# Retention stage: split products for the weighing, tiles long and short by turns, turning and gating one step later

## Chip, cores and metric

One Trainium2 chip, one core. The time is the device time of one execution in microseconds, of the program that computes three layers of a network for 1024 tokens. The change touches one stage of it, the retention.

## What is computed

For each of four heads, q and k (1024 x 256) are projected from the normed input and rotated, v (1024 x 512) is projected, and a gate g likewise. Then:

```python
s = einsum('qd,kd->qk', q, k) * gamma_h ** (t_q - t_k)    # for t_k <= t_q, else 0; k scaled by 256 ** -0.5
y = s @ v
y = (y - mean(y)) * rsqrt(var(y) + 1e-6)                  # per row of 512
y = y * silu(g)
```

The reference works in chunks of 128 with a carried state; the kernel computes the same sum over all earlier tokens directly. All inputs are fp32.

## The kernel before

The stage is `retention_stage`. Each head is a round: projections of q, k, v and gate (TensorE, as *split products*: an operand a is held as a_hi, rounded to fp32r, and a_lo = a - a_hi, and a product is three fp32r matmuls, hi*hi, hi*lo, lo*hi, in `product`, lines 773 to 781); then the scores and the weighing; and then the next head. GpSimd splits the arriving weights in slots (`w_split`, lines 730 and 732). Tokens are in eight tiles of 128.

In the weighing part, with key tile j and query tile i:

- `scores(j)` (L2914) multiplies key tile j with all queries from tile j on, in fp32, up to 512 columns at a time, into banks 0 and 1 or 2 and 3 of PSUM. VectorE's `decay(j)` (L3031) multiplies them by the decay table into the fp32 buffer `weights`. An fp32 matmul shows as two records in the trace.
- The weighing of query tile i (L2938) is i + 1 fp32 matmuls of 512 columns into bank 6 or 7. The tiles go in order, from one block to eight.
- VectorE takes the row statistics (L3050, L3054, L3056), ScalarE the root by Ln and Exp (L2980, L2982), VectorE a Newton step (L3061 to L3067) and the normed rows `yn` (L3072). TensorE turns them (`turn_y`, L2923) into bank 4 or 5, VectorE multiplies by the gate (`gated_out`, L3037) into `yT`. ScalarE stores `yT` at the end of the head.
- TensorE's order per head: scores 0 and 1, then for each tile i its weighing, scores i + 2, and the turn of tile i - 1; after tile 7, the first part of the next head's q projection (`narrow`, L777 to L781), and behind that the turn of tile 7. In VectorE's step i: statistics, decay(i + 2), Newton, normed rows of i, gate-out of i - 1.

In the last head, ScalarE (`rows_hi`, L2592), GpSimd (`rows_lo`, L2596) and SP's queue (`rows_load`) also bring the rows of the first two heads back in for the output projection, one k tile at a time in two buffers; before them GpSimd splits the next stage's first two weight slots (L2841, L2843). Engines run their queues in order and wait on counting semaphores. All wait counts are written by hand.

Of the kernel before, what the change touches and what calls it, by code (L numbers as in the profile page):

```python
# [85 lines left out]
def program(nc, x, positions, attn_norm_g, w_in, q_a_norm_g, w_q_b, kv_a_norm_g, w_kv_b, sb_out_norm_g,  # L86
# [2705 lines left out]
    def retention_stage(stage, weight, w, after):  # L2792
# [8 lines left out]
        tmp = sb("tmp", [P, 2, HALF])  # L2801
# [7 lines left out]
        yT = sb("yT", [P, NV, SEQ])  # L2809
        off = [sum((TT - i) * P for i in range(j)) for j in range(TT + 1)]  # L2810
        PA = sb("weights", [P, off[TT]])
# [3 lines left out]
        S = [ps[:, 0:2, :].rearrange("p b c -> p (b c)"), ps[:, 2:4, :].rearrange("p b c -> p (b c)")]  # L2815
        block = nc.Block()
        with block:
            @block.sync
            def _(sp):
                sp.dma_start(COS[:], tables["ret_cos"]).then_inc(gain_in.sem, 16)  # L2820
                sp.dma_start(SIN[:], tables["ret_sin"]).then_inc(gain_in.sem, 16)
                w_load_all(sp, w, RET_HEADS, per, ret_unit(weight), True)

                sp.wait_ge(w_lo.sem, w_lo.at(RET_HEADS * per + w.slots))
                for u in range(w.slots):
                    for dst, src in after(0, u)(w.raw[:, u, :]):
                        sp.dma_start(dst, src).then_inc(w_raw[u].sem, 16)
                sp.wait_ge(stored.sem, stored.at(16 * 2))
                rows_load(sp, ROWS)
# [19 lines left out]
            def _(pe):  # L2849
# [16 lines left out]
                for it in range(RET_HEADS):  # L2866
                    for u in range(1, 4):
                        if it and u == 2:

                            pe.wait_ge(y_out.sem, y_out.at(TT * it))  # L2870
                        narrow(it, u)

                    def values(u):

                        w_arrived(pe, w, it, per, u)
                        s = u % w.slots
                        for kk in range(2):
# [24 lines left out]

                    def scores(j):

                        if j < 2:

                            pe.wait_ge(dense_out.sem, dense_out.at(16 * it + 8 + 2 * j + 2))
                        else:
                            pe.wait_ge(decayed.sem, decayed.at(TT * it + j - 1))
                        n = (TT - j) * P  # L2910
                        for c0 in range(0, n, HALF):
                            c1 = min(c0 + HALF, n)
                            for i in range(2):
                                last = nc.tensor.matmul(S[j % 2][:, c0:c1], K[:, i, j * P:j * P + P],  # L2914
                                                        Q[:, i, j * P + c0:j * P + c1], start=i == 0, stop=i == 1)
                        last.then_inc(scores_ready.sem, 1)

                    def turn_y(i):
                        pe.wait_ge(normed.sem, normed.at(TT * it + i + 1))
                        if i >= 2:  # L2920
                            pe.wait_ge(y_out.sem, y_out.at(TT * it + i - 1))
                        for c in range(NV):
                            last = nc.tensor.transpose(ps[:, 4 + i % 2, c * P:c * P + P],  # L2923
                                                       YN[:, i % 2, c * P:c * P + P], ident[:])
                        last.then_inc(y_turned.sem, 1)

                    scores(0)
                    scores(1)
                    for i in range(TT):
                        pe.wait_ge(decayed.sem, decayed.at(TT * it + i + 1))  # L2930
                        if i == 0:
                            pe.wait_ge(dense_out.sem, dense_out.at(16 * it + 16))
                        if i >= 2:

                            pe.wait_ge(normed.sem, normed.at(TT * it + i - 1))
                        for j in range(i + 1):
                            at = off[j] + (i - j) * P
                            last = nc.tensor.matmul(ps[:, 6 + i % 2, :], PA[:, at:at + P], V[:, j, :],  # L2938
                                                    start=j == 0, stop=j == i)
                        last.then_inc(pv_done.sem, 1)  # L2940
                        if i + 2 < TT:
                            scores(i + 2)
                        if i >= 1:
                            turn_y(i - 1)
# [6 lines left out]
            def _(act):  # L2951
                for it in range(RET_HEADS):
                    act.dma_start(DEC[:], tables["decay"][bass.ds(it, 1), :, :].rearrange("a p c -> (a p) c"))\
                        .then_inc(table_in.sem, 16)
                    for i, t in enumerate(TOKENS):
                        act.wait_ge(dense_done.sem, dense_done.at(24 * it + 8 + i + 1))
                        nc.scalar.activation(V[:, t, :], ps[:, t, :], ACT.Copy).then_inc(dense_out.sem, 1)
                    for j in range(NV):
# [15 lines left out]
                        nc.scalar.activation(GE[:], GE[:], ACT.Ln, bias=1.0).then_inc(gate_exp.sem, 1)  # L2974
                        act.wait_ge(gate_step.sem, gate_step.at(2 * (NV * it + j) + 1))
                        nc.scalar.activation(GE[:], GE[:], ACT.Exp).then_inc(gate_exp.sem, 1)
                    for i in range(TT):
# [4 lines left out]
                        nc.scalar.activation(st[:, 10:11], st[:, 9:10], ACT.Exp, scale=-0.5).then_inc(root.sem, 1)  # L2982
                        for k in ROWS_AT[i] if it == RET_HEADS - 1 else ():
# [3 lines left out]
                    act.dma_start(YT[bass.ds(it * NV, NV), :, :].rearrange("a p t -> p a t"), yT[:])\  # L2987
# [3 lines left out]
            def _(dve):  # L2991
                dve.wait_ge(gain_in.sem, gain_in.at(32))
                with dve.Fori(0, RET_HEADS) as it:
# [29 lines left out]

                    for j in range(NV - 1):
# [3 lines left out]
                    def decay(j):  # L3028
                        n = (TT - j) * P
                        dve.wait_ge(scores_ready.sem, scores_ready.at(TT * it + j + 1))  # L3030
                        nc.vector.tensor_tensor(PA[:, off[j]:off[j] + n], S[j % 2][:, 0:n], DEC[:, 0:n], ALU.mult)\  # L3031
                            .then_inc(decayed.sem, 1)

                    def gated_out(i):
                        at = slice(i * P, i * P + P)
                        dve.wait_ge(y_turned.sem, y_turned.at(TT * it + i + 1))
                        nc.vector.tensor_tensor(yT[:, :, at], ps[:, 4 + i % 2, :].rearrange("p (v c) -> p v c", c=P),  # L3037
                                                GT[:, :, at], ALU.mult).then_inc(y_out.sem, 1)

                    decay(0)  # L3040
                    decay(1)
                    gate(NV - 1)

                    dve.wait_ge(stored.sem, stored.at(16 * it))
                    for i in range(TT):
                        st = stat[:, i, :]
                        o = ps[:, 6 + i % 2, :]
# [9 lines left out]
                        if i + 2 < TT:  # L3057
                            decay(i + 2)
# [15 lines left out]
                        if i >= 1:  # L3074
                            gated_out(i - 1)
# [10 lines left out]
        for m in (scores_ready, decayed, pv_done, ln_done, root, normed, y_turned, y_out):  # L3086
# [98 lines left out]
```

## Time and profile before

| | us |
|---|---|
| three runs, median (lowest, highest) | 3862.47 (3861.24, 3871.61) |
| the profiled execution | 3866.34 |
| its span | 3864.6 |
| mean granted TensorE clock | 0.966 |

The profile is of one execution. Times in the trace count from the start of its span. In a line of the timeline stand start, length, engine, line of the kernel, operation and tiles, and in brackets the idle time ahead and what ended it; several equal instructions in a row are merged (x16). The length of a matmul's record is longer than the distance to the next one, since matmuls are pipelined.

### The profile page before, as it was taken

How to read it: one execution, taken by the hardware profiler on the slowest of the kernel's cores; microseconds unless marked ns; L12 is line 12 of the kernel's file. 1: busy time of each engine (PE TensorE's matmuls, PEld its weight loads, DVE VectorE, ACT ScalarE, POOL GpSimd, SP SyncE). 2: the span in 40 equal slices, each digit the busy share in tenths (PEclk: the TensorE clock that was granted, in tenths of full speed). 3: DMA queues.
4: the chain of work that ended last, by engine and by line, in shares of the span. 5: the costliest groups of instructions: out<-in, count | busy, mean ns of one | idle time of the engine just before them, and what ended most of it. 6: DMA issues, size and time to landing. Idle time of an engine off the chain costs nothing. (4 is left out here: it accounts for less than half of the span.)

```text
span 3864.6 us, 48135 instructions
## 1 busy us (share of the span) xinstructions
PE 3640.7 (94%) x17390; PEld 2977.0 (77%) x17390; DVE 1636.6 (42%) x3174; ACT 1322.1 (34%) x2439; POOL 1387.1 (36%) x813
## 2 busy tenths in 40 slices
PE   7987798999999998999999999997899999999997
PEld 6776577878888886788888888886787776868686
DVE  4666445233333334465665655555103323241412
ACT  4777143111111113455555556656101203020300
POOL 3210300233333321455655665666322121313331
PEclk9997899999999998999999999998999999999998
DMA  3000201111111104342322432221413120202231
GB/s 93 23 6 6 52 31 65 45 60 50 49 50 48 46 27 92 41 57 47 52 55 47 37 41 39 36 36 50 147 33 110 33 66 28 71 23 76 92 127 70
DMA packets 200885, 208.25 MB, mean 54 GB/s; under 512 B 12360, under 2 KB 155759, under 8 KB 200703
## 3 DMA queue, kind: packets, MB, share of 16 engines
q1 hardware_dynamic: 181134, 154.70, 17.9%
q10 hardware_dynamic: 19568, 50.93, 3.7%
q8 instruction: 138, 2.26, 0.2%
q14 instruction: 45, 0.36, 0.0%
HBM read 174.08 MB, written 31.52 MB: 53 GB/s over the span
## 5 line engine op out<-in xcount | busy, mean ns | idle before, releaser
L777 PE MATMUL ps<-all_u_hi,kept_w_hi 128*128 128x512 f32 x1824 | 731.9, 401 | 21.7 <-POOL kept_w_lo L732 14.2
L781 PE MATMUL ps<-all_u_hi,kept_w_lo 128*128 128x512 f32 x1824 | 715.4, 392 | 0.0
L780 PE MATMUL ps<-all_u_lo,kept_w_hi 128*128 128x512 f32 x1824 | 714.2, 392 | 0.0
L730 POOL CAST kept_w_hi<-kept_w_raw 128x1024 fp32r<-128x1024 f32 x120 | 129.6, 1080 | 1396.5 <-PE ps L777 741.5
L1437 POOL TENSOR_SCALAR even_probs<-even_probs,even_stat 128x128 f32<-128x128 f32 (+7 forms) x256 | 450.8, 1769 | 295.4 <-DVE even_stat L1861 295.0
L777 PEld LDWEIGHTS ps<-all_u_hi,kept_w_hi 128*128 128x128 f32 x1824 | 347.0, 190 | 85.5 <-POOL kept_w_lo L732 14.4
L781 PEld LDWEIGHTS ps<-all_u_hi,kept_w_lo 128*128 128x128 f32 x1824 | 345.2, 189 | 74.5
L780 PEld LDWEIGHTS ps<-all_u_lo,kept_w_hi 128*128 128x128 f32 x1824 | 346.2, 190 | 63.4
L1866 DVE TENSOR_TENSOR even_probsT_lo<-ps,even_probsT_hi 128x512 fp32r<-128x512 f32 (+3 forms) x384 | 196.0, 551 | 262.8 <-ACT even_probsT_hi L1701 261.7
L1692 ACT ACTIVATE even_probs<-even_probs,even_stat 128x128 f32<-128x128 f32 (+7 forms) x256 | 199.1, 778 | 300.9 <-DVE even_stat L1855 300.9
L732 POOL TENSOR_TENSOR kept_w_lo<-kept_w_raw,kept_w_hi 128x1024 fp32r<-128x1024 f32 x120 | 294.5, 2454 | 9.6
L777 PE MATMUL ps<-kept_w_hi,all_u_hi 128*128 128x512 f32 x640 | 252.7, 395 | 8.3 <-DVEq L2673 8.3
L780 PE MATMUL ps<-kept_w_lo,all_u_hi 128*128 128x512 f32 x640 | 252.1, 394 | 0.0
L781 PE MATMUL ps<-kept_w_hi,all_u_lo 128*128 128x512 f32 x640 | 251.9, 394 | 0.0
L2758 ACT ACTIVATE mlp_relu<-ps 128x512 f32<-128x512 f32 x64 | 38.3, 598 | 575.4 <-PE ps L781 575.4
L1701 ACT ACTIVATE even_probsT_hi<-ps 128x512 fp32r<-128x512 f32 (+3 forms) x384 | 167.7, 488 | 50.6 <-PE ps L1553 41.4
L2782 DVE TENSOR_TENSOR residual<-ps,residual 128x512 f32<-128x512 f32 x128 | 87.4, 692 | 229.5 <-PE ps L781 229.5
L1553 PE MATMUL ps<-all_ident,even_probs 128*128 128x128 f32 x1152 | 164.8, 281 | 16.9 <-POOL even_probs L1437 12.8
L2684 DVE TENSOR_TENSOR residual<-ps,residual 128x512 f32 x48 | 32.7, 692 | 344.7 <-PE ps L781 344.7
L1553 PEld LDWEIGHTS ps<-all_ident,even_probs 128*128 128x128 f32 x1152 | 136.2, 144 | 33.1 <-POOL even_probs L1437 16.1
L1533 PE MATMUL ps<-even_k_hi_hi,even_q_hi_lo 128*128 128x512 f32 (+2 forms) x384 | 145.9, 382 | 6.5 <-DVE even_stat L1850 6.3
L1429 POOL TENSOR_TENSOR kept_w_lo<-kept_w_raw,kept_w_hi 128x1024 fp32r<-128x1024 f32 x62 | 149.1, 2405 | 5.3
(439 smaller groups left out, 7383.5 us busy)
## 6 DMA issues: line engine op xcount, KB each, us to landing
kept_w_raw<-in_even_w_in_dram SPq DMA_DIRECT2D x64, 512.0 KB, 7.7
kept_w_raw<-in_odd_w_in_dram SPq DMA_DIRECT2D x48, 512.0 KB, 3.7
kept_w_raw<-in_w_up_dram SPq DMA_DIRECT2D x16, 512.0 KB, 4.1
mlp_w_raw<-in_w_up_dram SPq DMA_DIRECT2D x16, 512.0 KB, 4.1
kept_w_raw<-in_w_down_dram SPq DMA_DIRECT2D x16, 512.0 KB, 3.5
mlp_w_raw<-in_w_down_dram SPq DMA_DIRECT2D x16, 512.0 KB, 3.5
scratch_h<-residual SPq DMA_DIRECT2D x2, 4096.0 KB, 14.2
even_bias<-scratch_negc ACTq DMA_DIRECT2D x16, 512.0 KB, 5.9
```

The costliest lines, as they stand in the source:

```text
L730: nc.gpsimd.tensor_copy(w.hi[:, s, :], w.raw[:, s, :]).then_inc(w_hi.sem, 1)
L732: nc.gpsimd.tensor_tensor(w.lo[:, s, :], w.raw[:, s, :], w.hi[:, s, :].bitcast(F32), ALU.subtract).then_inc(w_lo.sem, 1)
L777: ins = nc.tensor.matmul(dst, lh, rh, start=first, stop=False)
L780: nc.tensor.matmul(dst, lh, rl, start=False, stop=False)
L781: return nc.tensor.matmul(dst, ll, rh, start=False, stop=last)
L1429: nc.gpsimd.tensor_tensor(w.lo[:, s, :], w.raw[:, s, :], w.hi[:, s, :].bitcast(F32), ALU.subtract).then_inc(w_lo.sem, 1)
L1437: nc.gpsimd.tensor_scalar(PB[g % 2][:, at], PB[g % 2][:, at], inv[:, s:s + 1], None, ALU.mult)\
L1533: nc.tensor.matmul(S[s % 2][:, c0:c1], QHL[:, hh, at], KHH[:, hh, c0:c1], start=True, stop=False)
L1553: last = nc.tensor.transpose(T[n % 2][:, i * P:i * P + P], PB[g % 2][:, at:at + P], ident[:])
L1692: nc.scalar.activation(z, z, ACT.Exp, bias=nb[:, s:s + 1], accum_out=tot[:, s:s + 1])\
L1701: nc.scalar.activation(PTH[:, n % RING, c0:HALF], T[n % 2][:, c0:HALF], ACT.Copy)\
L1866: nc.vector.tensor_tensor(PTL[:, n % RING, c0:HALF], T[n % 2][:, c0:HALF], PTH[:, n % RING, c0:HALF].bitcast(F32), ALU.subtract)\
```

## The change

In the weighing the fp32 matmuls become split products: V is kept as `v_hi` and `v_lo`, and so are the decayed scores (ScalarE rounds with `weights_hi`, VectorE subtracts with `weights_lo`). Scores are now computed per query tile in pieces of 128 columns, since only two and a half tiles of split weights are kept. The tiles go in the order 7, 0, 6, 1, 5, 2, 4, 3. Three regions of PSUM hold scores (the third, bank 4, for short tiles), banks 5 and 6 the outputs, and bank 7 alone the turned rows. A tile's turn and gate-out come two steps after its weighing instead of one; the turn of the seventh tile stands ahead of the next head's projection. The gate's buffer takes the output in place, the rotation's temporaries lie in the gate's exponent buffer, and the last head's rows in the rotation tables.

```diff
-        rows = sb("rows", [P, 2, SEQ])
-        ROWS = (rows[:, 0, :], rows[:, 1, :])
+        ROWS = (COS[:], SIN[:])
-        V = sb("v", [P, TT, RET_V])
+        VH, VL = sb("v_hi", [P, TT, RET_V], FR), sb("v_lo", [P, TT, RET_V], FR)
+        tmp = GE.rearrange("p (i c) -> p i c", i=2)
+        WH, WL = (sb(name, [P, 2 * SEQ + HALF], FR) for name in ("weights_hi", "weights_lo"))
+        DS = sb("decayed", [P, 2 * SEQ + HALF])
+        ORDER = (7, 0, 6, 1, 5, 2, 4, 3)
+        ASKED = (0, 2, 1, 4, 3, 6, 5, 7)
+        ASK_AFTER = {0: 4, 1: 3, 2: 6, 3: 5, 5: 7}
...
+        S = [ps[:, 0:2, :].rearrange("p b c -> p (b c)"), ps[:, 2:4, :].rearrange("p b c -> p (b c)"), ps[:, 4, :]]
...
                 sp.wait_ge(stored.sem, stored.at(16 * 2))
+                sp.wait_ge(rot_step.sem, rot_step.at(24 * RET_HEADS))
                 rows_load(sp, ROWS)
...
-                            pe.wait_ge(dense_out.sem, dense_out.at(16 * it + TOKENS.index(n) + 1))
+                            pe.wait_ge(v_out_dve.sem, v_out_dve.at(TT * it + TOKENS.index(n) + 1))
...
+                    def scores(n):
...
+                            before = n - 4 if n % 2 == 0 else n - 2
+                            pe.wait_ge(decayed.sem, decayed.at(TT * it + asked(before)))
+                        t = ORDER[n]
+                        at = slice(t * P, t * P + P)
+                        for d in range(t + 1):
+                            key = slice((t - d) * P, (t - d) * P + P)
                             for i in range(2):
+                                last = nc.tensor.matmul(scores_of(n)[:, d * P:d * P + P], K[:, i, key], Q[:, i, at],
+                                                        start=i == 0, stop=i == 1)
...
+                    def turn_y(n):
+                        pe.wait_ge(normed.sem, normed.at(TT * it + n + 1))
+                        if n:
+                            pe.wait_ge(y_out.sem, y_out.at(TT * it + n))
...
+                    def weigh(n):
+                        pe.wait_ge(split_lo.sem, split_lo.at(TT * it + asked(n)))
...
+                        if n >= 2:
+
+                            pe.wait_ge(normed.sem, normed.at(TT * it + n - 1))
+                        t = ORDER[n]
+                        for d in range(t + 1):
+                            at = slice(part(n).start + d * P, part(n).start + d * P + P)
+                            last = product(output_of(n), (WH[:, at], WL[:, at]), (VH[:, t - d, :], VL[:, t - d, :]),
+                                           d == 0, d == t)
                         last.then_inc(pv_done.sem, 1)
+
+                    for n in ASKED[:3]:
+                        scores(n)
+                    for n in range(TT):
+                        weigh(n)
+                        if n in ASK_AFTER:
+                            scores(ASK_AFTER[n])
+                        if n >= 2:
+                            turn_y(n - 2)
+                    turn_y(TT - 2)
                     if it + 1 < RET_HEADS:
                         narrow(it + 1, 0)
                     turn_y(TT - 1)
...
+                        if j == NV - 1:
+                            weights_hi(ASKED[0])
                         act.wait_ge(gate_step.sem, gate_step.at(2 * (NV * it + j) + 1))
                         nc.scalar.activation(GE[:], GE[:], ACT.Exp).then_inc(gate_exp.sem, 1)
+                    for n in ASKED[1:3]:
+                        weights_hi(n)
...
+                        if i in ASK_AFTER:
+                            weights_hi(ASK_AFTER[i])
                         for k in ROWS_AT[i] if it == RET_HEADS - 1 else ():
                             rows_hi(act, ROWS, k)
...
+                    decay(ASKED[0])
+                    weights_lo(ASKED[0])
+                    decay(ASKED[1])
+                    decay(ASKED[2])
                     gate(NV - 1)
+                    weights_lo(ASKED[1])
+                    weights_lo(ASKED[2])
                     for i in range(TT):
...
+                        if i in ASK_AFTER:
+                            decay(ASK_AFTER[i])
...
+                        if i in ASK_AFTER:
+                            weights_lo(ASK_AFTER[i])
+                        if i >= 2:
+                            gated_out(i - 2)
+                    gated_out(TT - 2)
                     gated_out(TT - 1)
```

The lower half of V is made by VectorE (bank minus `v_hi`, eight times a head) ahead of the gates, and ScalarE waits for the last head's store before it evicts the first gate.

## Rows read from the trace of the kernel before

**Rows 1.** Page, part 1: busy time, share of the span, instructions.
```profile
PE 3640.7 (94%) x17390; PEld 2977.0 (77%) x17390; DVE 1636.6 (42%) x3174; ACT 1322.1 (34%) x2439; POOL 1387.1 (36%) x813
```

**Rows 2.** Busy by stretch, first head's weighing: length, PE, PEld, DVE, ACT, POOL, clock, DMA.
```profile
3055.90:3106.60 50.70, 49.84 (x151) 25.14 (x149) 28.58 (x73) 7.66 (x19) 0.00 (x0) 1.00 0.00 0
```

**Rows 3.** Timeline, TensorE, first head: start, length, engine, line, operation.
```profile
3056.12 6.60 PE L2914 MATMUL ps<-ret_q,ret_k 128*128 128x512 f32 x16
...
3070.91 0.66 PE L2923 MATMUL ps<-all_ident,ret_yn 128*128 128x128 f32 x4 [0.86 <-DVE ret_yn L3072]
...
3092.04 0.61 PE L2914 MATMUL ps<-ret_q,ret_k 128*128 128x128 f32 x4
...
3099.37 7.03 PE L2938 MATMUL ps<-ret_v,ret_weights 128*128 128x512 f32 x16
...
3106.59 0.48 PE L777 MATMUL ps<-all_u_hi,kept_w_hi 128*128 128x512 f32 x1
```

**Rows 4.** Timeline, TensorE, projection of V: the first matmuls of two neighbouring split products.
```profile
3005.12 0.39 PE L777 MATMUL ps<-kept_w_hi,all_u_hi 128*128 128x512 f32 x1
...
3005.80 0.39 PE L777 MATMUL ps<-kept_w_hi,all_u_hi 128*128 128x512 f32 x1
```

**Rows 5.** Narrow fp32 matmuls of another stage: its line's weight loads (ns), one timeline run.
```profile
L2395 PEld LDWEIGHTS ps<-latent_v,mla_probsT x288: 186/192/193, 541.6 to 642.7; 128*128 128x128 f32 x144
...
612.70 1.05 PE L2395 MATMUL ps<-latent_v,mla_probsT 128*128 128x128 f32 x8
```

**Rows 6.** Groups by line, VectorE and ScalarE, whole span: busy us, mean ns, idle before.
```profile
L2525 DVE TENSOR_TENSOR all_u_lo<-ps,all_u_hi 128x512 fp32r<-128x512 f32 x8 | 5.4, 680 | 0.0
L3031 DVE TENSOR_TENSOR ret_weights<-ps,ret_decay 128x1024 f32<-128x1024 f32 x4 | 4.9, 1225 | 27.3 <-PE ps L2914 27.3
L2246 DVE TENSOR_TENSOR all_u_lo<-latent_k_rope,all_u_lo 128x1024 fp32r<-128x1024 f32 x1 | 1.2, 1225 | 1.4 <-ACT all_u_lo L2220 1.4
...
L2592 ACT ACTIVATE all_u_hi<-ret_rows 128x1024 fp32r<-128x1024 f32 x8 | 8.2, 1044 | 3.6 <-DMA ret_rows<-scratch_yt 3.6
```

**Rows 7.** Timeline, VectorE, last head: the last tile's statistics, normed rows, last gate-out.
```profile
3655.63 0.70 DVE L3050 BATCH_NORM_STATS2 ret_stat<-ps 128x6 f32<-128x512 f32 x1 [3.40 <-PE ps L2938]
...
3658.13 0.81 DVE L3072 TENSOR_SCALAR ret_yn<-ps,ret_stat 128x512 f32<-128x512 f32 x1
...
3659.69 0.69 DVE L3037 TENSOR_TENSOR ret_yT<-ps,ret_gT 128x512 f32<-128x512 f32 x1 [0.15 <-PE ps L2923]
```

**Rows 8.** Timelines of VectorE and GpSimd, last head and the stage behind it.
```profile
3629.47 4.86 POOL L2596 TENSOR_TENSOR all_u_lo<-ret_rows,all_u_hi 128x1024 fp32r<-128x1024 f32 x2 [2.14 <-ACT all_u_hi L2592]
...
3632.28 2.07 DVE L3067 TENSOR_TENSOR ret_stat<-ret_stat 128x1 f32<-128x1 f32 x1
...
3675.82 1.04 POOL L730 CAST kept_w_hi<-kept_w_raw 128x1024 fp32r<-128x1024 f32 x1 [22.42 <-PE ps L777]
...
3676.11 1.83 DVE L2677 TENSOR_TENSOR wr_y_lo<-wr_y_raw,wr_y_hi 128x1024 fp32r<-128x1024 f32 x1 [1.51 <-ACT wr_y_hi L2667]
```

**Rows 9.** Timelines, start of the last head's weighing: TensorE's first scores, GpSimd's last weight split.
```profile
3605.32 6.60 PE L2914 MATMUL ps<-ret_q,ret_k 128*128 128x512 f32 x16
...
3610.28 2.35 POOL L2843 TENSOR_TENSOR kept_w_lo<-kept_w_raw,kept_w_hi 128x1024 fp32r<-128x1024 f32 x1
```

**Rows 10.** Busy by stretch, around waits of TensorE; columns as in rows 2.
```profile
275.60:279.00 3.40, 0.74 (x6) 0.50 (x5) 2.45 (x2) 3.32 (x6) 0.00 (x0) 1.00 0.00 0
279.00:283.00 4.00, 4.00 (x27) 3.45 (x28) 1.22 (x2) 1.68 (x5) 0.00 (x0) 1.00 0.00 0
110.80:114.20 3.40, 0.74 (x4) 0.58 (x4) 2.96 (x3) 3.30 (x6) 0.00 (x0) 1.00 0.00 0
114.20:117.60 3.40, 3.40 (x15) 3.02 (x14) 0.71 (x1) 0.00 (x0) 0.00 (x0) 0.50 0.00 0
...
3655.80:3661.40 5.60, 0.89 (x7) 0.44 (x5) 3.60 (x10) 0.41 (x2) 0.00 (x0) 0.94 0.02 7
3661.40:3667.40 6.00, 5.99 (x14) 4.74 (x15) 0.00 (x0) 0.00 (x0) 0.00 (x0) 0.50 1.01 345
```

More of the change, by code:

```diff
@@ L2800, in retention_stage, with part, asked @@
         SIN = sb("sin", [P, SEQ])
-        tmp = sb("tmp", [P, 2, HALF])
-        rows = sb("rows", [P, 2, SEQ])
-        ROWS = (rows[:, 0, :], rows[:, 1, :])
+        ROWS = (COS[:], SIN[:])
         ROWS_AT = ((), (0, 1), (2,), (3,), (4, 5), (6,), (7,), ())
         TOKENS = (0, 2, 1, 3, 4, 6, 5, 7)
-        V = sb("v", [P, TT, RET_V])
+        VH, VL = sb("v_hi", [P, TT, RET_V], FR), sb("v_lo", [P, TT, RET_V], FR)
         GT = sb("gT", [P, NV, SEQ])
         GE = sb("ge", [P, SEQ])
-        yT = sb("yT", [P, NV, SEQ])
-        off = [sum((TT - i) * P for i in range(j)) for j in range(TT + 1)]
-        PA = sb("weights", [P, off[TT]])
+        tmp = GE.rearrange("p (i c) -> p i c", i=2)
[4 more added lines that the diff above has]
+        ASK_AFTER = {0: 4, 1: 3, 2: 6, 3: 5, 5: 7}
+        def part(n):
+            start = n // 2 % 2 * SEQ if n % 2 == 0 else 2 * SEQ
+            return slice(start, start + (ORDER[n] + 1) * P)
+        def asked(n):
+            return ASKED.index(n) + 1
         DEC = sb("decay", [P, SEQ])
@@ L2901, in _ @@
                         wide(u)
-                    def scores(j):
-                        if j < 2:
-                            pe.wait_ge(dense_out.sem, dense_out.at(16 * it + 8 + 2 * j + 2))
-                        else:
[L2909 to L2912, printed above, removed]
+                    def scores(n):
+                        if n < 3:
+                            pe.wait_ge(dense_out.sem, dense_out.at(16 * it + 8 + {0: 2, 2: 4, 1: 5}[n]))
+                        else:
+                            before = n - 4 if n % 2 == 0 else n - 2
[4 more added lines that the diff above has]
+                            key = slice((t - d) * P, (t - d) * P + P)
@@ L2929, in _ @@
-                    for i in range(TT):
-                        pe.wait_ge(decayed.sem, decayed.at(TT * it + i + 1))
-                        if i == 0:
-                            pe.wait_ge(dense_out.sem, dense_out.at(16 * it + 16))
[L2933 to L2939, printed above, removed]
-                        last.then_inc(pv_done.sem, 1)
[L2941 to L2944, printed above, removed]
+                    def weigh(n):
+                        pe.wait_ge(split_lo.sem, split_lo.at(TT * it + asked(n)))
+                        if n == 0:
+                            pe.wait_ge(dense_out.sem, dense_out.at(16 * it + 16))
+                        if n >= 2:
[5 more added lines that the diff above has]
+                                           d == 0, d == t)
+                        last.then_inc(pv_done.sem, 1)
@@ L2956, in _, with weights_hi @@
                         act.wait_ge(dense_done.sem, dense_done.at(24 * it + 8 + i + 1))
-                        nc.scalar.activation(V[:, t, :], ps[:, t, :], ACT.Copy).then_inc(dense_out.sem, 1)
+                        nc.scalar.activation(VH[:, t, :], ps[:, t, :], ACT.Copy).then_inc(dense_out.sem, 1)
+                    def weights_hi(n):
+                        act.wait_ge(decayed.sem, decayed.at(TT * it + asked(n)))
+                        nc.scalar.activation(WH[:, part(n)], DS[:, part(n)], ACT.Copy).then_inc(split_hi.sem, 1)
+                    act.wait_ge(stored.sem, stored.at(16 * it))
                     for j in range(NV):
@@ L3022, in gate @@
                             .then_inc(gate_step.sem, 1)
+                    for i, t in enumerate(TOKENS):
+                        dve.wait_ge(dense_out.sem, dense_out.at(16 * it + i + 1))
+                        nc.vector.tensor_tensor(VL[:, t, :], ps[:, t, :], VH[:, t, :].bitcast(F32), ALU.subtract)\
+                            .then_inc(v_out_dve.sem, 1)
                     for j in range(NV - 1):
@@ L3026, in _, with decay @@
                     dve.wait_ge(table_in.sem, table_in.at(16 * it + 16))
[L3028 to L3031, printed above, removed]
+                    def decay(n):
+                        dve.wait_ge(scores_ready.sem, scores_ready.at(TT * it + asked(n)))
+                        cs = (ORDER[n] + 1) * P
+                        nc.vector.tensor_tensor(DS[:, part(n)], scores_of(n)[:, 0:cs], DEC[:, 0:cs], ALU.mult)\
@@ L3085, in retention_stage @@
         gate_step.close(2 * NV * R_)
-        for m in (scores_ready, decayed, pv_done, ln_done, root, normed, y_turned, y_out):
+        for m in (v_out_dve, split_hi, split_lo, scores_ready, decayed, pv_done, ln_done, root, normed, y_turned, y_out):
             m.close(TT * R_)
```

43 lines of the change are left out of this document (18 added, 25 removed).

## Prediction

> **What bounds the kernel now.** I read the page first: TensorE is busy for 94% of the span, VectorE 42%, ScalarE 34%, GpSimd 36% [rows 1]. So a change counts where it alters what TensorE does or waits for. The end of the chain of waits holds only the final norm, which isn't touched. Next, the table of stretches. From a head's first scores to the next head's first projection takes 50.47 us (3056.12 to 3106.59), in which TensorE is busy 49.8 of 50.7 [rows 2, 3]. Then the order of instructions on TensorE in that stretch. Its one wait is for tile 0's normed rows, 0.86 us in the view and 1.03 by issue [rows 3]. In the last head 50.3 us pass from first score (3605.32) to the last tile's statistics (3655.63) [rows 7, 9], and in the first the last weighing ends 50.1 after the first score [rows 3]: one walk serves for all. I call 0 the start of the first score matmul.
>
> **TensorE's own work, per head.** An fp32 matmul is two records here. Sixteen of 512 columns take 7.03 us, the last one's 0.59 being its own length: (7.03 - 0.59)/15 = 0.429 each [rows 3]. So one weighing block costs 0.858 us. A split product is three fp32r matmuls, and one follows the other every 0.68 us (3005.12 to 3005.80) [rows 4]. 36 blocks: 30.9 before, 24.5 after, **-6.4 us**.
>
> The scores stay fp32, but are now computed tile by tile in pieces of 128 columns: 36 blocks x 2 halves of the channels x 2 records = 144, where there were 48 of up to 512 columns, 15.4 us in all (72 pieces of 128 columns x 2 records x 0.429/4). Four records of 128 columns take 0.61 us, the last one's 0.275 included: 0.112 each [rows 3]; eight in a row, each with its own load, take 1.05: 0.111 [rows 5]. So 144 x 0.112 = 16.1: **+0.7 us**. The turns are unchanged, 7 x 0.44 = 3.1 in this stretch. Work: 49.4 before, 43.7 after, 5.7 less per head.
>
> The weight load is what could spoil this. Its record lasts 0.19 us, longer than the 0.112 between matmuls, and 288 loads stand beside 288 matmuls [rows 5]: they overlap. The Trainium skill (TensorE: Matmul & The Clock Gate, Part 3: Packing small matmuls, The mechanism) says that a weight load overlaps running matmuls only when it goes to another group of rows. By that rule the loads of these full-array matmuls would not be hidden, and the sum would be that of rival D. The rows at 0.111 disagree with it, and they decide.
>
> **VectorE and ScalarE gain work.** Per tile the decayed scores now go to an fp32 buffer (same multiply as before, 1.23 us for 1024 columns), ScalarE rounds them (1.04 for 1024), VectorE subtracts (1.23 for 1024 with both operands in SBUF) [rows 6]. V's lower half is 8 subtractions of 0.68 [rows 6] and its upper half the old copy; they lie at the start of the gate projections, where each bank is needed 5.4 us after the other. Cost nothing there; with that cover gone 0.68 a tile. The wait for the stored rows moves from VectorE to ScalarE, in front of the gate evictions, some 80 us of projections after the store was issued; were the store slower than those, the evictions would wait out the rest. The last rows' loads wait for the rotation, done 100 us earlier; nothing. The aliases (temporaries in the gate buffer, output in place) add no wait that is not already in engine order. Aliased rows keep their order on SP's queue: behind them nothing but the next stage's weights.
>
> **The hand-overs, walked.** TensorE now waits for each tile's lower split. The turned rows have one bank in place of two: turn n waits for gate-out n-1. And that gate-out comes on VectorE one step later, behind the norm of tile n+1. I walked the queues step by step with durations from rows: operations on VectorE follow each other 0.09 us before their recorded ends, a dependent one 0.03 to 0.04 after, TensorE starts 0.06 after its releaser. The same walk on the old order gives 50.53 for the next projection (measured 50.47) and 1.06 for the wait (1.03), and for the last head 55.0 to its last gate-out (measured 3659.69 + 0.69 - 3605.32 = 55.06) [rows 7, 9].
>
> New order, heads 1 to 3, tiles in order 7, 0, 6, 1, 5, 2, 4, 3. Scores end at 7.16; decay, rounding and subtraction of tile 7 end at 7.38: wait 0.3. Weighing 0 is followed by short work (one block, two of scores), while VectorE is still held by the gate and two subtractions until 13.4: wait 1.1 for the norm of the first tile before the third weighing. Second turn 0.7, fifth 0.4, sixth 0.55. The last weighing ends at 45.6. Then the **seventh turn** needs the sixth tile's gate-out, and VectorE does that only behind the whole chain of the eighth tile. That chain takes 3.31 us from statistics to end of norm (3655.63 to 3658.13 + 0.81) [rows 7], then 0.6 for the gate-out: turn at 49.9, wait 3.27 behind a turn of 0.44. Only then comes the next head's projection, which before ran while this chain was worked. It starts at **50.4, 0.1 earlier than before**: the 5.7 us of work saved go to the waits (0.3 + 1.1 + 0.7 + 0.4 + 0.55 + 3.3 = 6.4, less the old 1.0) and to five restarts of 0.06.
>
> **Last head.** Here GpSimd works beside it. A VectorE multiply of a single column with both operands in SBUF lasted 2.07 us, until GpSimd's subtraction ended; a subtraction of 1024 columns that began under a GpSimd cast took 1.83 in place of 1.23 [rows 6, 8]. So they exclude each other. Before, these were paid under long weighings. The new subtractions have both operands in SBUF: the first finds GpSimd splitting the next stage's weights until 3612.63, 7.3 after the first score [rows 9]: 1.2 later. In the middle, the walk meets GpSimd's eight row subtractions (4.86 a pair [rows 8]) three more times with 0.5 to 2.3 each; waits of 1.6, 2.05 and 1.9 at the second, third and fifth turns. The last weighing ends at 51.1, the last gate-out at 58.4: **+3.4 us** against 55.0. With no GpSimd there it would be 52.7, -2.3. The Trainium skill (SBUF — State Buffer, SBUF: two separate sides) calls this an exclusive lock held for the whole instruction, for a VectorE operation with two SBUF inputs. The trace agrees, 2.07 and 1.83 us.
>
> **The clock.** TensorE ran at 2.4 GHz throughout the four heads, the single wait of 1.0 us included. At the end of the last head it was busy for 0.89 of 5.6 us, and then ran 6.0 us at 1.2 GHz (0.50) [rows 10], costing 3.0. In an earlier stage 0.74 busy of 3.4 us was followed by 3.4 us at 0.50, costing 1.7; the same 0.74 of 3.4 later on was followed by the full clock [rows 10]. The new wait of 3.3 with 0.55 before it is the same kind, in each of three heads: I take a fall each time and 2.3 us (between 1.7 and 3.0; 0 is rival B), and 0.4 for the last head, which has its fall already.
>
> **Sum.** 3 x (-0.1 + 2.3) + 3.4 + 0.4 = +10.4, by the unrounded walk +10.3. Own time of the profiled execution 3866.34 (span 3864.6 plus 1.7) gives 3876.6. It lies 3.87 above the median of the runs shown, 3862.47; so the forecast for the median is **3872.8**, +0.27%. About 0.3% (11.6 us) is what a measurement of this kernel tells from no change.
>
> **Rivals.**
> A, the forecast: waits as walked, one fall of the clock per head. The hand-over's bounds (0.02 less or 0.04 more at each release shift the walk by -2 and +4) and the fall's (1.7 or 3.0) make it 3867 to 3878. Chance 0.60.
> B, the clock stays at 2.4 GHz through these waits, as once in rows 10. 3 x (-0.1) + 3.4 = +3: 3865.5. For it: the lone case; against: the case at the end of the last head, the nearest in kind. 0.12.
> C, slower: the waits lie close enough together that the clock falls twice in a head, or in the last head at the turns with waits of 1.6 to 2.05 as well. Each further fall costs 1.7 to 3.0; three or more of them, +16 to +20: 3879 to 3883. It decides from the point at which waits near 2 us suffice. For it: the end of the last head in rows 10 was two waits, not one; against: the 1.0 us of rows 3 never did. 0.15.
> D, slower: the scores' loads do not hide. 96 more of them x 0.19 us [rows 5] = 18 us a head, 72 in all, of which some 12 would lie in the new waits: 10 + 72 - 12 = +70, 3932. Rows 5 speak against. 0.03.
> E, faster: the wait of 3.3 at the seventh turn does not come, the norm chain being covered. Then 3.3 + 2.3 drop from three heads and 3.3 from the last: 10.3 - 20 = -10, 3852. It needs TensorE to go past a waiting turn; nothing in the trace does. That the split products are not faster than fp32 is excluded by rows 4. 0.10.
>
> **Chances and range.** The bound of +11.6 is at 3874.1, with two fifths of A's 3867 to 3878 above it: 0.24 of 0.60 slower, 0.36 same. Same 0.36 + 0.12 (B) = 0.48; slower 0.24 + 0.15 + 0.03 = 0.42; faster 0.10 (E). The range 3857 to 3883 holds A, B and nearly all of C, and leaves out D and E (0.13) and a rest of C.
>
> **What would show it.** Right: weighing records in threes, 0.226 us apart, 108 a head; score records 0.112 apart; a wait of about 3.3 us before the seventh turn, put down to the gate-out; the next projection's first matmuls with granted clock 0.50; VectorE subtractions of the last head longer than their size. Wrong: the stretch of a head well off 50.4 us; projections at full clock (then B); more than one fall in a head (C); score pitch near 0.3 (D).

## The result, and the profile after

| | before | after |
|---|---|---|
| first series: median of 11 runs each, us | 3862.14 | 3878.50 |
| lowest to highest | 3855.97 to 3871.61 | 3870.08 to 3883.43 |
| profiled execution | 3866.34 | 3873.59 |
| its span | 3864.6 | 3871.8 |

The ratio is 1.0039, with a 95% interval of 1.003 to 1.0047: the change makes the kernel some 15 us slower (16.4 by the medians). A second series (12 runs of the unedited changed kernel beside 35 of the kernel before) gives 1.0028 (1.0019 to 1.0038), 3874.28 against 3862.94. The forecast was 3872.8. One of the twelve executions of the one-step kernel below took 11238 us and is left out of its ratio.

The stage is best compared inside a trace, from the first score matmul of the first head to the first matmul of the next stage. Before, that is 3661.41 - 3056.12 = 605.3 us; the start is in [rows 3], and this row of its timeline ends it:

```profile
3661.41 0.76 PE L777 MATMUL ps<-kept_w_hi,all_u_hi 128*128 128x512 f32 x1 [1.76 <-DVEq L2673]
```

After, 3670.30 - 3055.49 = 614.8: **9.5 us more**. These are TensorE's rows of the changed kernel's timeline, first head and the first matmul of the next stage; they answer to [rows 3].

```profile
3055.49 7.30 PE L2934 MATMUL ps<-ret_q,ret_k 128*128 128x128 f32 x64
...
3062.89 0.50 PE L777 MATMUL ps<-ret_v_hi,ret_weights_hi 128*128 128x512 f32 x1
...
3063.69 0.40 PE L777 MATMUL ps<-ret_v_hi,ret_weights_hi 128*128 128x512 f32 x1
...
3064.38 0.39 PE L777 MATMUL ps<-ret_v_hi,ret_weights_hi 128*128 128x512 f32 x1
...
3085.35 0.63 PE L2943 MATMUL ps<-all_ident,ret_yn 128*128 128x128 f32 x4 [1.01 <-DVE ret_gT L3082]
...
3098.64 0.63 PE L2943 MATMUL ps<-all_ident,ret_yn 128*128 128x128 f32 x4 [0.37 <-DVE ret_gT L3082]
...
3102.46 0.63 PE L2943 MATMUL ps<-all_ident,ret_yn 128*128 128x128 f32 x4 [0.45 <-DVE ret_gT L3082]
...
3106.27 0.63 PE L2943 MATMUL ps<-all_ident,ret_yn 128*128 128x128 f32 x4 [3.18 <-DVE ret_gT L3082]
...
3106.65 0.49 PE L777 MATMUL ps<-all_u_hi,kept_w_hi 128*128 128x512 f32 x1
...
3670.30 0.76 PE L777 MATMUL ps<-kept_w_hi,all_u_hi 128*128 128x512 f32 x1 [1.76 <-DVEq L2673]
```

64 narrow score records take 7.30 us, so (7.30 - 0.275)/63 = 0.112 each. Split products follow each other every 0.69 us once running (3063.69 to 3064.38); from the first to the second it is 0.80. Four turns wait for VectorE's gate-out (L3082), the second, fifth, sixth and seventh tile's; the seventh waits 3.18 us. The projection of the next head (L777) starts 3106.65 - 3055.49 = 51.16 after the first scores; before it was 50.47.

Ahead of the second turn (3085.35) VectorE pauses before the third tile's normed rows:

```profile
3083.06 0.81 DVE L3119 TENSOR_SCALAR ret_yn<-ps,ret_stat 128x512 f32<-128x512 f32 x1 [0.38 <-DVE ret_stat L3114]
```

VectorE at that seventh turn, same head. It answers to [rows 7]: statistics of the eighth tile, its normed rows, the sixth tile's gate-out.

```profile
3102.23 0.69 DVE L3097 BATCH_NORM_STATS2 ret_stat<-ps 128x6 f32<-128x512 f32 x1
...
3104.72 0.81 DVE L3119 TENSOR_SCALAR ret_yn<-ps,ret_stat 128x512 f32<-128x512 f32 x1
3105.45 0.68 DVE L3082 TENSOR_TENSOR ret_gT<-ps,ret_gT 128x512 f32<-128x512 f32 x1
```

The gate-out of a tile that was turned long ago stands 3.2 us behind the start of the next but one tile's statistics; the turn starts 0.14 after its end. And the clock, from the table of stretches (columns as in [rows 2]; it answers to [rows 10]):

```profile
3101.90:3106.70 4.80, 1.17 (x10) 0.88 (x9) 3.40 (x10) 0.41 (x2) 0.00 (x0) 1.00 0.00 0
3107.10:3110.50 3.40, 3.40 (x10) 2.63 (x9) 0.53 (x1) 0.00 (x0) 3.11 (x2) 0.50 0.00 0
3110.60:3114.00 3.40, 3.40 (x16) 2.81 (x15) 0.00 (x0) 0.00 (x0) 0.21 (x1) 1.00 0.50 154
```

After 1.17 us of work in 4.8, TensorE runs at 1.2 GHz for 3.4 us and then at 2.4 again. The second and third head have a fall of the same length, but it begins earlier, before the wait at the seventh turn is over:

```profile
3291.40:3294.80 3.40, 3.33 (x10) 2.88 (x11) 0.69 (x1) 0.00 (x0) 1.56 (x2) 0.51 0.02 5
3475.80:3479.10 3.30, 2.77 (x9) 2.42 (x10) 1.07 (x2) 0.00 (x0) 1.04 (x1) 0.50 0.02 5
```

In the last head, the timelines of TensorE, VectorE and GpSimd around the fifth turn; they answer to [rows 8]. L3108 is the first Newton multiply.

```profile
3651.86 2.40 POOL L2596 TENSOR_TENSOR all_u_lo<-ret_sin,all_u_hi 128x1024 fp32r<-128x1024 f32 x1 [0.49 <-ACT all_u_hi L2592]
...
3652.14 2.13 DVE L3108 TENSOR_TENSOR ret_stat<-ret_stat 128x1 f32<-128x1 f32 x1 [0.20 <-ACT ret_stat L3016]
3654.31 0.16 DVE L3110 TENSOR_TENSOR ret_stat<-ret_stat 128x1 f32<-128x1 f32 x1
...
3657.04 1.09 PE L2943 MATMUL ps<-all_ident,ret_yn 128*128 128x128 f32 x4 [2.64 <-DVE ret_gT L3082]
```

The multiply ends at 3654.27, 0.01 after GpSimd's subtraction; the fifth turn then waits 2.64 us, where the first head's waits 0.37. The last head's groups show the new subtractions: 2.29 us for 1024 columns, where 896 took 1.09, and 2.50 for 256 columns. Both began while GpSimd was at work and ended after it:

```profile
L3076 DVE TENSOR_TENSOR ret_weights_lo<-ret_decayed,ret_weights_hi 128x256 fp32r<-128x256 f32 x1 | 2.5, 2502 | 0.0
L3076 DVE TENSOR_TENSOR ret_weights_lo<-ret_decayed,ret_weights_hi 128x1024 fp32r<-128x1024 f32 x1 | 2.3, 2293 | 1.1 <-ACT ret_weights_hi L2985 1.1
...
L3076 DVE TENSOR_TENSOR ret_weights_lo<-ret_decayed,ret_weights_hi 128x896 fp32r<-128x896 f32 x1 | 1.1, 1085 | 0.0
```

### The profile page after: what moved, and what is told of

Its sections match the earlier page's. It is cut to its first block and busy times, and to the rows that moved or that the text cites. A ratio compares the mean times of both kernels' runs of the same rounds, so it can differ in the third digit from the quotient of the medians.

```text
span 3871.8 us, 49356 instructions
## 1 busy us (share of the span) xinstructions
PE 3626.5 (94%) x17918; PEld 3036.7 (78%) x17918; DVE 1677.1 (43%) x3238; ACT 1343.4 (35%) x2471; POOL 1388.7 (36%) x813
## 5 line engine op out<-in xcount | busy, mean ns | idle before, releaser
L777 PE MATMUL ps<-all_u_hi,kept_w_hi 128*128 128x512 f32 x1824 | 733.2, 402 | 21.9 <-POOL kept_w_lo L732 14.5
L777 PEld LDWEIGHTS ps<-all_u_hi,kept_w_hi 128*128 128x128 f32 x1824 | 347.6, 191 | 86.3 <-POOL kept_w_lo L732 14.7
L777 PE MATMUL ps<-kept_w_hi,all_u_hi 128*128 128x512 f32 x640 | 252.2, 394 | 8.3 <-DVEq L2673 8.3
L1701 ACT ACTIVATE even_probsT_hi<-ps 128x512 fp32r<-128x512 f32 (+3 forms) x384 | 167.7, 488 | 50.5 <-PE ps L1553 41.2
```

The lines of the kernel that those rows point to most:

```text
L777: ins = nc.tensor.matmul(dst, lh, rh, start=first, stop=False)
L1701: nc.scalar.activation(PTH[:, n % RING, c0:HALF], T[n % 2][:, c0:HALF], ACT.Copy)\
```

## The experiments

The theory: the split products save what they should, and the single turning bank, with the gate-out one step later, turns the saving into waits; the longest of these, at the end of a head, also lowers TensorE's clock; in the last head GpSimd lengthens VectorE's chain. Rivals: narrow scores or conversions cost it; the clock has nothing to do with the wait; the last head waits for its transfers.

**The changed kernel again** (no edit).

> The changed kernel once more, unedited. It gives a second set of its times and a second profiled execution. In the first one the stage lost 5.7 us in heads 1 to 3 and 3.8 in the last (9.5 in all), with one fall of TensorE's clock of 3.4 us in each of the first three heads and two in the last; its execution was 3873.6 us, while the median of the runs was 3878.5, with one group at 3870 to 3877 and one at 3881 to 3883. Theory: the waits are the same to 0.1 us each time, and what differs between executions is how many clock falls come after them and how long they are. Then this profile shows the same waits (3.3 us at the seventh turn) and again one fall or two per head, and the times again spread over some 10 us. Rival: the difference is outside the retention stage; then the stage is the same to 1 us and other stages differ.

The first head's waits are the same to 0.01 us, with the seventh turn again at 3.18:

```profile
3061.60 1.61 PE L2934 MATMUL ps<-ret_q,ret_k 128*128 128x128 f32 x13
...
3112.41 0.63 PE L2943 MATMUL ps<-all_ident,ret_yn 128*128 128x128 f32 x4 [3.18 <-DVE ret_gT L3082]
...
3676.52 0.76 PE L777 MATMUL ps<-kept_w_hi,all_u_hi 128*128 128x512 f32 x1 [1.76 <-DVEq L2673]
```

The stage took 3676.52 - 3061.60 = 614.9 us, the first time 614.8. The clock falls inside it were the same too; the whole difference, 6.1 us, was there before the first scores. So the rival of that expectation holds as to the place. But the falls in front of the stage do differ: the trace's clock record has 242.4 us at 1.2 GHz there, that of the first profile 232.1. These 10.3 us at half the clock can be up to 5.1 of the 6.1 (an estimate).

**The kernel before, again** (no edit).

> The kernel before, unedited, for a second profiled execution. The five profiles of kernels that are the same up to the retention stage start its first scores at 3050 to 3062 us. Theory: that spread is of the part in front of the stage and the same for all kernels; here the first scores lie somewhere between 3049 and 3063, and the stage itself takes what it took, 182.9 to 183.2 us a head, to 0.2 us. Rival (the change shifts the part in front, by its layout): the first scores of the kernel before come at 3056.1 to 0.5 us again.

```profile
3048.55 1.02 PE L2914 MATMUL ps<-ret_q,ret_k 128*128 128x512 f32 x2
...
3653.55 0.77 PE L777 MATMUL ps<-kept_w_hi,all_u_hi 128*128 128x512 f32 x1 [1.76 <-DVEq L2673]
```

Stage 605.0 us, first scores 7.6 us earlier than in the first profile of the same kernel just before the range that was expected. The rival, a layout that shifts the part in front, falls. Over all ten profiles, in which TensorE's work is the same up to there, the first scores lie between 3048.6 and 3063.5. The time at 1.2 GHz in front of them goes with it: 204.8 to 208.2 us in the three earliest, 228.7 to 242.4 in the three latest. So a single execution says little about the whole, and the stage's own length (within 0.3 us for each of the two kernels that were profiled twice) says much.

**Filling the wait**

```diff
+                    for _ in range(13):
+                        nc.tensor.matmul(ps[:, 4, 0:P], K[:, 0, 0:P], Q[:, 0, 0:P], start=True, stop=True)
                     turn_y(TT - 2)
```

> The changed kernel with 13 fp32 matmuls of 128 columns into a bank that is free by then (2.9 us of work, result unused) in front of the seventh turn, where TensorE waits 3.35 us. Nothing that anyone waits for is moved by it. Theory (the clock falls because of this wait and costs about 2 us a head): no fall in heads 1 to 3, the next head's projection starts where it did (51.2 us after the first scores), and the kernel gains 4 to 8 us against the changed one, so +4 to +10 against before. Rival (the fall comes from the many small waits, or costs nothing): falls stay and the time is that of the changed kernel, or up to 1 us more a head.

```profile
3101.96 3.07 PE L2970 MATMUL ps<-ret_q,ret_k 128*128 128x128 f32 x26
3105.30 0.63 PE L2943 MATMUL ps<-all_ident,ret_yn 128*128 128x128 f32 x4 [0.28 <-DVE ret_gT L3084]
3105.69 0.48 PE L777 MATMUL ps<-all_u_hi,kept_w_hi 128*128 128x512 f32 x1
```

And the stretch behind it, of the same kernel (columns as in [rows 2]):

```profile
3106.00:3116.00 10.00, 10.00 (x44) 8.30 (x43) 0.66 (x1) 0.00 (x0) 3.44 (x2) 1.00 0.18 54
```

In the first head the projection starts where it did (3105.69 against first scores at 3054.52: 51.17) and runs at 2.4 GHz; in the next two, where the fall used to begin before it, it starts 0.3 and 0.4 earlier. Useless work in the wait makes the kernel faster: the stage took 610.7 us, 4.1 less; the median is 3867.90 us against 3874.28 of the changed kernel beside it, ratio to before 1.0013 (1.0003 to 1.0023). A head lasts 183.9, 183.7 and 183.6 us in place of 185.4, 184.9 and 184.6: a fall costs 1.5, 1.2 and 1.0 us, not the 2.3 that I had put, and least where part of it lies in the wait. The smaller waits stayed and the falls went, so it is the long wait that brings them.

**The last two odd turns in a free bank**

```diff
-        TURN = ps[:, 7, :]
+        def turn_of(n):
+            return ps[:, 4 if n in (TT - 3, TT - 1) else 7, :]
...
-                        if n:
-                            pe.wait_ge(y_out.sem, y_out.at(TT * it + n))
+                        if n and n != TT - 3:
+                            pe.wait_ge(y_out.sem, y_out.at(TT * it + (n - 1 if n > TT - 3 else n)))
```

> The changed kernel with the sixth and the eighth turn written to the bank of the third score region, which is read for the last time before; everything else as it is. So the seventh turn waits for the fifth tile's gate-out and no longer for the sixth's behind the eighth tile's norm chain. Theory (the single turning bank with the gate-out one step later is what eats the gain): the next projection starts 46.6 us after a head's first scores in place of 51.2, no clock fall in heads 1 to 3, 3.9 us a head faster than before the change; the last head 1 to 2 us slower than before; in all -6 to -12 us against before, 0.997 to 0.998. Rival (the loss is in narrow scores, conversions or shared ports): the start moves by the bare 3.3 us or less and the kernel stays slower than before.

```profile
3049.95 7.30 PE L2936 MATMUL ps<-ret_q,ret_k 128*128 128x128 f32 x64
...
3096.38 1.21 PE L2945 MATMUL ps<-all_ident,ret_yn 128*128 128x128 f32 x8
3097.34 0.48 PE L777 MATMUL ps<-all_u_hi,kept_w_hi 128*128 128x512 f32 x1
```

The sixth and seventh turn now run as one row of eight records without a wait, and the projection starts 3097.34 - 3049.95 = 47.4 us after the scores (expected 46.6, by the walk, which was 0.8 early for the changed kernel too). That is 3.8 earlier than in the changed kernel, more than the rival's bare 3.3. No clock fall in the first three heads. Stage 595.8 us, 9.5 less than before the change and 19.0 less than with the change; ratio 0.9981 (0.997 to 0.9992). One more bank for two of the eight turns turns the loss into a gain of the same size.

**Gate-out one step after the weighing again**

```diff
-                        if n >= 2:
-                            turn_y(n - 2)
-                    turn_y(TT - 2)
+                        if n >= 1:
+                            turn_y(n - 1)
...
-                        if i >= 2:
-                            gated_out(i - 2)
-                    gated_out(TT - 2)
+                        if i >= 1:
+                            gated_out(i - 1)
```

> One part of the change undone: each tile is turned and gated one step after its weighing again, as before the change, with the seventh turn in its place after the eighth weighing; split products, order of tiles and the one turning bank stay. Theory: the gate-out no longer stands behind the next tile's chain, so at the end of a head no turn waits for it: next projection at 47.1 us, no fall of the clock, 3.5 us a head faster than before, last head 1.5 to 2.5 slower, in all -5 to -11 us. Rival (the later step pays, since it takes the turn's wait for the normed rows off TensorE): the waits move into the middle of the head, one in front of each turn, and the time is that of the changed kernel or more, +10 to +25.

```profile
3098.01 0.63 PE L2943 MATMUL ps<-all_ident,ret_yn 128*128 128x128 f32 x4 [0.45 <-DVE ret_gT L3081]
3098.39 0.48 PE L777 MATMUL ps<-all_u_hi,kept_w_hi 128*128 128x512 f32 x1
```

With a single bank but the old step, the seventh turn waits 0.45 us; projection at 3098.39 - 3050.68 = 47.7. Stage 599.1 us, 6.2 less than before the change; ratio 0.998 (0.9971 to 0.9989). The rival (the later step pays) falls. So neither half of the pair, one bank or the later step, makes the kernel slower alone; it takes both.

**Weighing in fp32 again, in the new order**

```diff
-                            last = product(output_of(n), (WH[:, at], WL[:, at]), (VH[:, t - d, :], VL[:, t - d, :]),
-                                           d == 0, d == t)
+                            last = nc.tensor.matmul(output_of(n), DS[:, at], VH[:, t - d, :].bitcast(F32),
+                                                    start=d == 0, stop=d == t)
```

> One part of the change undone: the weighing is again one fp32 matmul per block (from the decayed scores and V's rounded half; V's lower half is left out of the product), in the new order, with all conversions and waits kept. Theory (the split products do save 0.18 us a block, 6.4 a head, and the waits are another matter): next projection 56 to 56.5 us after the first scores in place of 51.2, the same 3.3 us wait at the seventh turn and clock falls after it; in all 15 to 19 us slower than the changed kernel, +25 to +29 against before. Rival (the products bring nothing in this place, since waits for VectorE take their room): within 5 us of the changed kernel.

```profile
3113.49 1.09 PE L2943 MATMUL ps<-all_ident,ret_yn 128*128 128x128 f32 x4 [3.24 <-DVE ret_gT L3082]
3114.23 0.78 PE L777 MATMUL ps<-all_u_hi,kept_w_hi 128*128 128x512 f32 x1
```

Projection at 3114.23 - 3057.73 = 56.5, against 51.2 with split products; stage 632.5 us, 17.7 more than the changed kernel; ratio 1.0071 (1.0054 to 1.0087). The products do save: 5.3, 4.6 and 5.0 us of this stretch in the first three heads, less than the 6.4 of the sum, and 2.0 in the last. The wait at the seventh turn is about the same, 3.24: it follows VectorE's chain and not the kind of product.

**GpSimd's row subtractions of the last head cut to one column**

```diff
-                    rows_lo(pool, ROWS, k)
+                    pool.wait_ge(hi_done.sem, hi_done.at(k + 1))
+                    nc.gpsimd.tensor_tensor(UL[:, k, 0:1], ROWS[k % 2][:, 0:1], UH[:, k, 0:1].bitcast(F32),
+                                            ALU.subtract).then_inc(lo_done.sem, 1)
```

> The changed kernel with GpSimd's eight row subtractions beside the last head cut to one column each (the lower half of those rows is left out, so the output projection works with rounded rows). ScalarE's copies, the transfers and everything else stay. Theory (the last head loses because VectorE's small multiplies and new subtractions, both operands in SBUF, and GpSimd's subtractions exclude each other): the 2.7 us wait of TensorE before the fifth turn falls to the 0.5 of the other heads, the last gate-out ends 53.9 to 54.5 us after the first scores in place of 58.9, heads 1 to 3 are unchanged, the kernel is 4 to 5 us faster than the changed one. The 1.3 us wait in front of the first weighing stays, for it is GpSimd's weight split. Rival (the last head waits for row transfers or ScalarE's copies): the last gate-out stays within 1 us of 58.9.

TensorE, last head, fifth to eighth turn:

```profile
3663.68 0.63 PE L2945 MATMUL ps<-all_ident,ret_yn 128*128 128x128 f32 x4 [0.36 <-DVE ret_gT L3084]
3667.50 0.63 PE L2945 MATMUL ps<-all_ident,ret_yn 128*128 128x128 f32 x4 [0.43 <-DVE ret_gT L3084]
3671.31 1.09 PE L2945 MATMUL ps<-all_ident,ret_yn 128*128 128x128 f32 x4 [3.18 <-DVE ret_gT L3084]
3673.28 1.08 PE L2945 MATMUL ps<-all_ident,ret_yn 128*128 128x128 f32 x4 [0.88 <-DVE ret_gT L3084]
...
3676.12 0.77 PE L777 MATMUL ps<-kept_w_hi,all_u_hi 128*128 128x512 f32 x1 [1.76 <-DVEq L2673]
```

The fifth turn's wait falls from 2.64 to 0.36. The last gate-out ends 55.4 us after the head's scores, where 53.9 to 54.5 was expected and 58.9 was measured with the full subtractions. The shortfall is that the clock now falls within these turns (records of 1.08 where 0.63 is usual), so part of what was won was given back. The last head is 3.5 us shorter, but the stage only 2.2 (4 to 5 was expected): the third head had a fall of 6.8 us in place of 3.4 and took 186.1 in place of 184.6. The kernel: ratio to before 1.0011 (1.0001 to 1.0021), 3870.28 us; the rival (transfers, copies) falls.

**Together**: one step, the free bank, and in the first tile's step VectorE's multiply of the next scores behind the normed rows. Only this third edit is shown; the other two are those above.

```diff
-                        if i in ASK_AFTER:
+                        if i in ASK_AFTER and i:
                             decay(ASK_AFTER[i])
                         v, r, q = st[:, 8:9], st[:, 10:11], st[:, 11:12]
...
+                        if not i:
+                            decay(ASK_AFTER[i])
```

> Three edits to the changed kernel together: gate-out one step after the weighing again, the sixth and eighth turn in the free bank, and in the first tile's step VectorE's multiply of the next scores moved behind the normed rows, since there it waits 1.1 us for those scores while the norm chain stands behind it. Theory: the wait of 1.1 to 1.2 us before the second tile's turn or the third weighing goes, and no turn waits at the end of a head: next projection at 45.3 to 46.2 us against 50.5 before the change, last head 0.5 to 2.5 us slower than before; in all -9 to -15 us, ratio 0.996 to 0.998, 3 to 4 us below each of the two earlier variants. Rival (VectorE is full there, so the wait only moves to the next turn): no better than the two variants, -5 to -9 us.

```profile
3060.19 7.30 PE L2936 MATMUL ps<-ret_q,ret_k 128*128 128x128 f32 x64
...
3077.43 0.60 PE L2945 MATMUL ps<-all_ident,ret_yn 128*128 128x128 f32 x4
...
3089.24 0.63 PE L2945 MATMUL ps<-all_ident,ret_yn 128*128 128x128 f32 x4 [1.01 <-DVE ret_gT L3083]
...
3105.66 0.66 PE L2945 MATMUL ps<-all_ident,ret_yn 128*128 128x128 f32 x4 [0.28 <-DVE ret_yn L3120]
3106.08 0.49 PE L777 MATMUL ps<-all_u_hi,kept_w_hi 128*128 128x512 f32 x1
...
3651.69 0.76 PE L777 MATMUL ps<-kept_w_hi,all_u_hi 128*128 128x512 f32 x1 [1.76 <-DVEq L2673]
```

The first turn (3077.43) waits for nothing; the third still waits 1.01, where the same edit for the third tile's step would apply (not tried). Projection at 3106.08 - 3060.19 = 45.9. Stage 591.5 us, 13.8 less than before; 3851.78 us, **ratio 0.9964 (0.9951 to 0.9977)**: it beats both kernels. The heads are 4.5 to 5.0 us shorter than before in the first three, where the sum of the work promised 5.7, and the last one 0.7 longer. What each of the three edits adds beside the other two was not measured.

| | next projection, head 1 | stage | ratio to before |
|---|---|---|---|
| before (two profiles) | 50.5 | 605.3, 605.0 | 1 |
| changed (two profiles) | 51.2 | 614.8, 614.9 | 1.0039, 1.0028 |
| changed, wait filled | 51.2 | 610.7 | 1.0013 |
| changed, free bank | 47.4 | 595.8 | 0.9981 |
| changed, one step | 47.7 | 599.1 | 0.998 |
| changed, fp32 weighing | 56.5 | 632.5 | 1.0071 |
| changed, last rows cut | 51.2 | 612.7 | 1.0011 |
| together | 45.9 | 591.5 | 0.9964 |

The ratios stand in three series, each with its own runs of the kernel before: the first 1.0039; 1.0028 and the next three kernels; and the last three.

## Why the prediction came out as it did

The time lay in the range and the mechanism was rival A's, the forecast: 3878.50 in the first series, 5.7 above it, and 3874.28 in the second. The stage alone lost 9.5 us where 10.3 was forecast. That this is so near is in part luck, since two errors of about 3 us cancelled: the heads' projections started later than said, and the clock's falls cost less. Point by point:

- **Work.** Score records 0.112, as said. Rival D, the loads that don't hide, falls: 64 in a row at 0.112 with a load each. The Trainium skill (TensorE: Matmul & The Clock Gate, Part 3: Packing small matmuls, The mechanism) has the sentence that a load overlaps only when it goes to another group of rows; the trace speaks against that sentence, while the same section also lets a load into a background weight buffer go ahead. The split products of the first head's 36 blocks took 25.4 us in place of 24.5, since the first of each weighing takes 0.77 to 0.80 to the next one. But the turns and scores ahead are shorter by nearly as much (a turn 0.35 to 0.38, not 0.44). In all the stretch holds 44.1 us of work, where the walk had 44.0 with its restarts.
- **Hand-overs.** Here lies the difference between 50.4 and 51.2. Waits in the first head by issue, said and found: first weighing 0.3 and 0.26, third weighing 1.1 and 1.2, second turn 0.7 and 1.2, fifth 0.4 and 0.5, sixth 0.55 and 0.6, seventh 3.27 and 3.35; in all 6.4 and 7.1. Most of it is the second turn. Ahead of it VectorE pauses 0.38 us before the third tile's normed rows, where the same step follows after 0.03 to 0.04 in the second and eighth tile; why is open. The walk's step that decided, the seventh turn behind the eighth tile's chain, held in every kernel that kept it.
- **Clock.** One fall in each of the first three heads, as said, so rival B falls; but each lasted 3.4 us, and the filled wait prices them at 1.0 to 1.5 us, not 2.3. Over three heads that was 3.2 us too much. The projections, 0.7 to 0.8 us later than before the change instead of 0.1 earlier, gave back 2.6 of it.
- **Last head.** Said +3.8 with its clock share; from its first scores (3610.39) to the next stage 59.9 us against 56.1 [rows 9: start 3605.32]: +3.8. The pieces differ: VectorE's work was lengthened at one Newton multiply (2.13) and at the subtractions of 1024 and 256 columns. TensorE waited 1.19, 0 and 2.64 us at the second, third and fifth turns, where the walk had 1.6, 2.05 and 1.9. The last gate-out ended at 58.9, not 58.4.
- **Sum.** Heads 1 to 3 lost 2.6, 1.7 and 1.4 us (said 2.2 each), in all 9.5 in the stage against 10.3. Rival A's range of 3867 to 3878 doesn't follow from its own terms: -2 and 3 x -0.6 below 10.3, +4 and 3 x 0.7 above it, give 3869 to 3879. The first median lies in this one and just above the one that I gave.
- **The rest.** The medians differ by 16.4 us in one series and 11.3 in the other, the stage by 9.5. TensorE's work is the same up to the first scores, and there the profiled executions spread over 15 us. In the second series the median granted clock is 0.965 with the change and 0.968 without. By the clock records of the two first profiles the stage has 17.1 us at 1.2 GHz in place of 0.7, which makes 0.002 of the 0.003. In the 35 executions of the kernel before, 0.001 of clock goes with about 2.2 us, and 1.8 are left to explain in this series (an estimate from a correlation). Why more time at 1.2 GHz should lie outside the stage with the change isn't shown, and the 7 us of the first series stay open. The first series lies above 0.3%, the second below; I had 0.48 for within 0.3% and 0.42 for slower.
- Rivals C (a second fall in a head) and E (the wait doesn't come) did not occur in heads 1 to 3; the last head did have one fall in its middle, at the fifth turn's wait, which is one of C's places.

## What to carry to other kernels

When a buffer goes from two to one, follow the step that frees it to its place in the other engine's queue: here a gate-out that was ready stood behind 3.3 us of another tile's chain, and either a second bank or the earlier place was enough to turn the loss into a gain. A saving on the bounding engine counts less the waits that it opens, so walk the queues with the measured durations before trusting the sum of the work. Compare kernels by the stage inside the trace where whole executions spread more than the effect.

## What the runs showed of the hardware

Useless work in a wait can pay: 2.9 us of matmuls, 26 records, in the longest wait of each head kept TensorE at 2.4 GHz behind it in the first three heads and saved 4.1 us over the stage, though the wait itself was not shortened. A fall of 3.4 us cost 1.5 us where it began after the wait, and 1.0 to 1.2 where it began before the wait was over. The first split product behind scores or a turn takes 0.77 to 0.80 to the next one and not 0.68, with a wait before it or without; the turn ahead of it is shorter by 0.1, so it is no dearer work. And a VectorE multiply of a single column can cost 2.13 us in place of 0.16 where GpSimd runs a long operation on SBUF: the size of a two-operand step beside GpSimd says little of what it costs; the Trainium skill (SBUF — State Buffer, SBUF: two separate sides) tells it as an exclusive lock, and the end times in the last head, 0.01 us apart, agree.
